# Two moves in the order of work of an expert loop: one on VectorE, one on ScalarE

## The chip, the cores and the metric

The kernel runs on one core of a Trainium2 chip. The metric is the device time of one execution in microseconds (us). Five engines take part: TensorE (PE in the profile, with its weight loads as PEld), VectorE (DVE), ScalarE (ACT), GpSimd (POOL) and SyncE (SP), which here only issues transfers. Each works through its own list of instructions in order and waits on semaphores for the others.

## What is computed

One layer of an encoder for 512 tokens of 2048 numbers: two kinds of attention and a recurrence side by side, a cross attention, and a mixture of experts. The change touches the experts alone, which are, with 32 experts of 512 inner features and two experts per token:

```
def expert_block(args):
    tok, e = args
    xb = x_pad[tok]
    a = jax.nn.silu(xb @ w_gate[e]) * (xb @ w_up[e])
    return a @ w_down[e]
...
y_rows = y_rows.reshape(n_rows, D) * row_w[:, None].astype(y_rows.dtype)
y = jax.ops.segment_sum(y_rows, row_tok, num_segments=N + 1)[:N]
```

All is float32. Each expert has 12 MB of weights and on average 32 rows of tokens.

## The kernel before

**The pieces.** An expert's weights come as 12 pieces of 128 x 2048 numbers, 1 MB each, numbered r: 0 to 3 gate, 4 to 7 up, 8 to 11 down. So the "first gate piece" is r = 0 and the "fourth" is r = 3. Pieces 8 and 9 (`RAW_ONLY`) are multiplied as they land, in float32. The other ten are split in two parts first: ScalarE copies `e_raw` to a rounded `e_hi` (L1399), and VectorE subtracts, `e_lo = e_raw - e_hi` (L1860). TensorE multiplies by both (L1035 and L1036 for gate and up, L1066 and L1067 for down). Both splits are the functions `e_split(b, r)` of the two engines, b being the expert.

**The buffers.** `e_raw`, `e_hi` and `e_lo` have five buffers each for the ten split pieces (`RING = 5`), and `e_raw` has two more for pieces 8 and 9. Piece r of gate and up shares its buffer with piece r - 5, pieces 10 and 11 have those of 3 and 4. SP issues all transfers of weights in one fixed order (L490): before one it waits until VectorE has subtracted the earlier piece of that buffer (`e_lo_done`), and so piece 5 waits for piece 0, and pieces 6 and 7 for 1 and 2. Transfers that are issued queue up and land in that order.

**A round.** The engines run `expert(b, behind, ahead)` for 32 experts, the middle ones in a hardware loop. The order of each engine is written out by hand. The down product of expert b - 1 is worked off in the round of expert b (`behind`), and the first pieces of expert b + 1 are split in it (`ahead`). TensorE's order is: pieces 0 to 5; the transposes of the next expert's rows (L1020); the gate result folded (L1043); pieces 6 and 7; down piece 8 of b - 1 (L1063); the up result folded; down pieces 9, 10 and 11 of b - 1.

**What the change touches.** VectorE's `gate_times_up(b)` forms the product `he` (L1957) from the folded results. It has three waits: `he_silu` from ScalarE, `up_folded` from TensorE, and `e_used` up to piece 9 of b - 1, since TensorE still reads the old `he` for pieces 8 and 9. VectorE's `y_add(b - 1)` adds two halves of the down result into `y_sb` (L1969), one of which ScalarE's `y_low(b - 1)` has copied out of PSUM (L1443). GpSimd then scatters `y_sb` to memory (L657) and gathers the rows of a later expert (L645). On ScalarE `y_low` waits until TensorE has used piece 11. `split_he` makes the parts of `he` that the split down pieces need (L1437, L1962).

Of the kernel before, what the change touches and what calls it, by code (L numbers as in the profile page):

```python
# [63 lines left out]
def layer(nc, x, mem, norm_mix_g, w_in, kv_norm_g, k_idx_norm_g, w_uk, w_uv, conv_w, conv_b, gate_b,  # L64
          ml_norm_g, w_out, norm_x_g, mem_norm_g, w_cq, w_ckv, w_co, norm_ffn_g, w_group, b_group,
          w_router, b_router, w_gate, w_up, w_down, final_norm_g, out):
    with ExitStack() as ctx:
# [85 lines left out]
        def small(name, shape, dt=F32):  # L153
            n = int(np.prod(shape[1:])) * 4
            t = at(name, shape, low[0], dt)
            low[0] += ((n + 31) // 32 * 32) / KB
            assert BASE + low[0] * KB <= nc.sbuf_usable_end, (name, low[0])
            return t
# [71 lines left out]
        more = small("more", [P, NE])  # L230
# [113 lines left out]
        def raw_at(b, r):  # L344
            return e_raw[RAW_LAST[r] if is_last_down(b, r) else RAW[r]]
# [4 lines left out]
        def slot_at(b, r):  # L350
            return SLOT_LAST[r] if is_last_down(b, r) else SLOT[r]
# [17 lines left out]
        def split_count(b, r, more=False):  # L369

            n = r if r < 8 else r - 2
            if more or is_last_down(b, r):
                return b * 10 + (n + 1)
            if r >= 8:
                return b * 10 + (n + 9)
            return n + 1 if isinstance(b, int) and b == 0 else b * 10 + (n - 1)

        def used_count(b, r, more=False):

            if more or is_last_down(b, r):  # L380
                return b * 12 + (r + 1)
            if r >= 8:
                return b * 12 + (r + 9)
            return r + 1 if isinstance(b, int) and b == 0 else b * 12 + (r - 3)
# [718 lines left out]
        def _(act):  # L1103
# [277 lines left out]
            def e_split(b, r, more=False):  # L1381

                act.wait_ge(land_at(b, r), landed(b, r, more))
                first_ = isinstance(b, int) and b == 0 and r < 8
                if first_ and r == 3:
                    act.wait_ge(slot_land, 32)
                    act.wait_ge(more_done, 1)
                    for k in range(2):
                        act.wait_ge(h_store[k], 16 * TT // 2)
                if is_last_down(b, r):  # L1390
                    act.wait_ge(e_used, used_count(b, r - 5))
                elif r >= 8:
                    act.wait_ge(e_used, used_count(b, r - 7, True) if more else used_count(b + 1, r - 7))
                elif r >= RING:
                    act.wait_ge(e_used, used_count(b, r - RING, more))
                elif not first_ and not more:
                    act.wait_ge(e_used, used_count(b - 1, r + RING) if r < 3 else b * 12 + (r - 8))
                n = slot_at(b, r)
                act.activation(e_hi[n][:, :], raw_at(b, r)[:, :], ACT.Copy).then_inc(e_hi_done, 1)  # L1399
# [15 lines left out]
            def rows_out(b):  # L1415

                act.wait_ge(xg_turned, b + 1)
                for k in range(2):
                    act.activation(xt_pair[:, 8 * k:8 * k + 8, 0:BLOCK], psx[2 + k][:, :].rearrange("p (k s) -> p k s", k=8),
                                   ACT.Copy).then_inc(xt_high, 1)  # L1420

            def gate_up(b, more=False):
                for r in range(3, 6):
                    e_split(b, r, more)
                act.wait_ge(e_used, used_count(b, 3, more))
                if not (isinstance(b, int) and b == 0):
                    act.wait_ge(he_done, b)
                act.activation(gu_sb[:, 0, :], psx[0][:, :], ACT.Copy).then_inc(gate_out, 1)
                for r in (6, 7):
                    e_split(b, r, more)  # L1430
                act.wait_ge(gate_folded, b + 1)
                act.activation(he_g[:, :, :], psx[0][:, 0:FT * BLOCK].rearrange("p (f s) -> p f s", f=FT),
                               ACT.Silu).then_inc(he_silu, 1)

            def split_he(b):
                act.wait_ge(he_done, b + 1)
                act.activation(he_pair[:, :, 0:BLOCK], he[:, :, 0:BLOCK], ACT.Copy).then_inc(he_split_a, 1)  # L1437

            def y_low(b, more=False):
                act.wait_ge(e_used, used_count(b, 11, more))  # L1440
                act.wait_ge(put_copied, b + 1)
                for m in range(4):
                    act.activation(y_sb[:, 512 * m:512 * m + 512], psd[m][BLOCK:P, :], ACT.Copy).then_inc(y_low_out, 1)  # L1443

            def expert(b, behind, ahead):
                gate_up(b)
                if behind:
                    e_split(b - 1, 10)
                if ahead:
                    act.wait_ge(e_used, used_count(b, 7))  # L1450
                    rows_out(b + 1)
                if behind:
                    e_split(b - 1, 11)
                if ahead:
                    for r in range(3):
                        e_split(b + 1, r)
                if behind:
                    y_low(b - 1)
                split_he(b)

            rows_out(0)
            expert(0, False, True)
            with act.Fori(1, LAST) as b:
                expert(b, True, True)
            expert(LAST, True, False)
            for r in (10, 11):
                e_split(LAST, r)
# [23 lines left out]
        def _(dve):  # L1491
# [365 lines left out]
            def e_split(b, r, more=False):  # L1857
                dve.wait_ge(e_hi_done, split_count(b, r, more))
                n = slot_at(b, r)
                dve.tensor_tensor(e_lo[n][:, :], raw_at(b, r)[:, :], e_hi[n][:, :].bitcast(F32),  # L1860
                                  ALU.subtract).then_inc(e_lo_done, 1)
# [78 lines left out]
            def rows_out(b):  # L1940
                for k in range(2):
                    dve.wait_ge(xt_high, b * 2 + (k + 1))
                    dve.tensor_tensor(xt_pair[:, 8 * k:8 * k + 8, BLOCK:P],
                                      psx[2 + k][:, :].rearrange("p (k s) -> p k s", k=8),
                                      xt_pair[:, 8 * k:8 * k + 8, 0:BLOCK].bitcast(F32), ALU.subtract).then_inc(xg_out, 1)

            def up_scaled(b, more=False):
                dve.wait_ge(e_used, used_count(b, 7, more))
                dve.tensor_scalar(gu_sb[:, 1, :], psx[1][:, :], slots[:, span(b, 1), 2:3].rearrange("s b c -> s (b c)").bitcast(F32),
                                  None, ALU.mult).then_inc(up_out, 1)  # L1950

            def gate_times_up(b, more=False):
                if not (more or isinstance(b, int) and b == 0):
                    dve.wait_ge(e_used, used_count(b - 1, 9))
                dve.wait_ge(he_silu, b + 1)
                dve.wait_ge(up_folded, b + 1)
                dve.tensor_tensor(he[:, :, 0:BLOCK], psx[1][:, 0:FT * BLOCK].rearrange("p (f s) -> p f s", f=FT),  # L1957
                                  he_g[:, :, :], ALU.mult).then_inc(he_done, 1)

            def split_he(b):  # L1960
                dve.wait_ge(he_split_a, b + 1)
                dve.tensor_tensor(he_pair[:, :, BLOCK:P], he[:, :, 0:BLOCK], he_pair[:, :, 0:BLOCK].bitcast(F32),  # L1962
                                  ALU.subtract).then_inc(he_split_d, 1)

            def y_add(b):
                for m in range(4):
                    dve.wait_ge(y_low_out, b * 4 + (m + 1))
                    y_m = y_sb[:, 512 * m:512 * m + 512]
                    dve.tensor_tensor(y_m, psd[m][0:BLOCK, :], y_m, ALU.add).then_inc(y_out, 1)  # L1969

            def expert(b, behind, ahead):
                for r in range(3, 8):
                    e_split(b, r)
                if behind:
                    e_split(b - 1, 10)
                up_scaled(b)
                if ahead:
                    rows_out(b + 1)
                if behind:
                    e_split(b - 1, 11)  # L1980
                gate_times_up(b)
                if ahead:
                    for r in range(3):
                        e_split(b + 1, r)
                if behind:
                    y_add(b - 1)
                split_he(b)
# [4 lines left out]
            with dve.Fori(1, LAST) as b:  # L1992
                expert(b, True, True)
# [75 lines left out]
```

## Time and profile before

| | us |
|---|---|
| median of 3 runs | 2683.26 |
| lowest and highest | 2680.72 and 2683.41 |
| the profiled execution, its own time | 2688.69 |
| its span, first to last instruction | 2686.9 |
| TensorE busy | 2408.5 |
| VectorE busy | 1529.3 |
| ScalarE busy | 1208.6 |
| GpSimd busy | 319.0 |

The span begins with the dense projections and attention, up to about 1540 us; the experts fill the rest but for the last 60 us. Busy shares over the whole span mix these stages, so the experts have to be read by views of their own stretch. The page cuts the span into 40 slices of 67 us. A digit is the busy share of a slice in tenths. "PEclk" is the granted clock of TensorE in tenths of 2.4 GHz. "GB/s" is what the transfers moved in each slice.

### The profile page before, as it was taken

To read this page: it belongs to the slowest core of one execution; us is meant where nothing else is said; L and a number is where in the kernel's file an instruction comes from. 1 tells how busy PE (TensorE), PEld (TensorE's weight loads), DVE (VectorE), ACT (ScalarE), POOL (GpSimd) and SP (SyncE) were. 2 spreads that over 40 slices of the span, in tenths; PEclk is the share of its full clock that TensorE was granted. 3 is DMA by queue.
4 is the path that set the end of the run, shared out by engine and by line. 5 is a ranking of instruction groups with operands and counts; after the bars stand their busy time and mean duration, and the time that the engine had idled before them with its cause. 6 is when DMAs were issued, how large, how long until landed. Compare 5 with 4: busy or idle time off the path is not lost.

```text
span 2686.9 us, 31537 instructions
## 1 busy us (share of the span) xinstructions
PE 2408.5 (90%) x11141; PEld 1888.5 (70%) x11141; DVE 1529.3 (57%) x1704; ACT 1208.6 (45%) x1376; POOL 319.0 (12%) x182
## 2 busy tenths in 40 slices
PE   6999999899998999999998389999999999999980
PEld 6888588667886889995887266666666666666660
DVE  4322476644234234443233577878887778877775
ACT  4222333443222223443222266666666666666651
POOL 0000000000000000000000122222222222222222
PEclk8999999999998999999999599999999999999995
DMA  4333133103222225650324399999999999999985
GB/s 172 99 96 100 40 97 99 47 24 126 100 88 110 100 93 151 181 163 20 111 94 171 89 371 375 385 381 383 392 385 387 382 383 380 387 380 380 384 326 208
DMA packets 141956, 580.31 MB, mean 216 GB/s; under 512 B 24394, under 2 KB 26704, under 8 KB 86736
## 3 DMA queue, kind: packets, MB, share of 16 engines
q1 hardware_dynamic: 136528, 562.85, 56.6%
q0 software_dynamic: 5376, 16.81, 1.9%
q8 instruction: 28, 0.46, 0.1%
q14 instruction: 24, 0.20, 0.0%
HBM read 571.15 MB, written 25.23 MB: 222 GB/s over the span
## 4 chain that ended last, share of the span: by engine, by line
PE 73%; DVE 17%; issue 6%; DMA 2%; ACT 1%; POOL 0%; DVEq 0%; SPq 0%; POOLq 0%; ACTq 0%
PE psd L722 41%; PE psd L1063 8%; DVE e_lo L1860 8%; PE psx L1035 6%; PE psx L1036 6%; DVE y_sb L1969 3%; PE psx L1020 2%; PE psx L1043 2%; PE psd L970 1%; PE psx L951 1%; PE psd L897 1%; DVE act_lo L1565 1%; PE psd L860 1%; PE psx L786 1%; PE psx L827 1%
## 5 line engine op out<-in xcount | busy, mean ns | idle before, releaser
L1860 DVE TENSOR_TENSOR e_lo<-e_raw,e_hi 128x2048 fp32r<-128x2048 f32 x320 | 718.8, 2287 | 127.0 <-ACT e_hi L1399 127.0
L1504 DVE TENSOR_TENSOR w_lo<-w_raw,w_hi 128x1024 fp32r<-128x1024 f32 (+1 forms) x240 | 291.0, 1213 | 661.0 <-ACT w_hi L1113 661.0
L1399 ACT ACTIVATE e_hi<-e_raw 128x2048 fp32r<-128x2048 f32 x320 | 595.5, 1910 | 32.8 <-DMA e_raw<-in_w_gate_dram 26.1
L1113 ACT ACTIVATE w_hi<-w_raw 128x1024 fp32r<-128x1024 f32 (+1 forms) x240 | 251.9, 1050 | 779.9 <-PE psd L722 779.9
L1035 PE MATMUL psx<-e_hi,xt_pair 128*128 128x512 f32 x1024 | 444.0, 434 | 92.6 <-DVE e_lo L1860 88.0
L1036 PE MATMUL psx<-e_lo,xt_pair 128*128 128x512 f32 x1024 | 429.3, 419 | 0.0
L1035 PEld LDWEIGHTS psx<-e_hi,xt_pair 128*128 128x128 f32 x1024 | 211.4, 206 | 169.7 <-DVE e_lo L1860 119.7
L722 PE MATMUL psd<-w_hi,act_hi 128*128 128x512 f32 (+1 forms) x832 | 320.6, 385 | 6.1 <-DVE act_lo L1565 2.1
L722 PE MATMUL psd<-w_lo,act_hi 128*128 128x512 f32 (+1 forms) x832 | 319.9, 384 | 0.0
L722 PE MATMUL psd<-w_hi,act_lo 128*128 128x512 f32 (+1 forms) x832 | 319.8, 384 | 0.0
L657 POOL DMA_INDIRECT y_rows<-y_sb,put_idx x32 | 208.5, 6515 | 619.0 <-DVE y_sb L1969 619.0
L1036 PEld LDWEIGHTS psx<-e_lo,xt_pair 128*128 128x128 f32 x1024 | 211.2, 206 | 43.7
L1063 PE MATMUL psd<-e_raw,he 128*128 128x512 f32 x512 | 233.3, 599 | 3.4 <-DVE y_sb L1969 3.4
L722 PE MATMUL psd<-act_hi,w_hi 128*128 128x512 f32 x576 | 225.0, 391 | 3.5 <-DVE act_lo L1565 2.0
L722 PE MATMUL psd<-act_hi,w_lo 128*128 128x512 f32 x576 | 224.9, 390 | 0.0
L722 PE MATMUL psd<-act_lo,w_hi 128*128 128x512 f32 x576 | 224.7, 390 | 0.0
L722 PEld LDWEIGHTS psd<-w_hi,act_hi 128*128 128x128 f32 x832 | 157.0, 189 | 37.7 <-issue 2.5
L722 PEld LDWEIGHTS psd<-w_hi,act_lo 128*128 128x128 f32 x832 | 156.9, 189 | 30.2
L722 PEld LDWEIGHTS psd<-w_lo,act_hi 128*128 128x128 f32 x832 | 156.9, 189 | 29.8
L1063 PEld LDWEIGHTS psd<-e_raw,he 128*128 128x128 f32 x512 | 95.3, 191 | 99.5 <-issue 97.1
L722 PEld LDWEIGHTS psd<-act_hi,w_hi 128*128 128x128 f32 x576 | 108.5, 188 | 26.8 <-DVE w_lo L1504 2.3
L722 PEld LDWEIGHTS psd<-act_lo,w_hi 128*128 128x128 f32 x576 | 108.6, 188 | 22.6
(302 smaller groups left out, 2964.9 us busy)
## 6 DMA issues: line engine op xcount, KB each, us to landing
e_raw<-in_w_gate_dram SPq DMA_DIRECT2D x128, 1024.0 KB, 10.7
e_raw<-in_w_up_dram SPq DMA_DIRECT2D x128, 1024.0 KB, 6.1
e_raw<-in_w_down_dram SPq DMA_DIRECT2D x128, 1024.0 KB, 9.8
w_raw<-in_w_in_dram SPq DMA_DIRECT2D x72, 512.0 KB, 3.6
w_raw<-in_w_ckv_dram SPq DMA_DIRECT2D x64, 512.0 KB, 3.6
w_raw<-in_w_out_dram SPq DMA_DIRECT2D x32, 512.0 KB, 3.6
w_raw<-in_w_cq_dram SPq DMA_DIRECT2D x32, 512.0 KB, 3.6
w_raw<-in_w_co_dram SPq DMA_DIRECT2D x32, 512.0 KB, 3.6
```

Source lines behind the costliest of these rows:

```text
L657: pool.indirect_dma_start(out=y_rows[:, :], out_offset=bass.IndirectOffsetOnAxis(ap=put_idx[:, 1:2], axis=0), in_=y_sb[:, :], in_offset=No ...
L722: ins = pe.matmul(o, a, c, start=(kt == 0 and q == 0), stop=(kt == KT - 1 and q == 2))
L1020: ins = pe.transpose(psx[2 + k // 8][:, BLOCK * (k % 8):BLOCK * (k % 8) + BLOCK], xg[:, k:D:KT], ident[0:BLOCK, 0:BLOCK])
L1035: pe.matmul(psx[u][:, :], pair, e_hi[SLOT[r]][:, c], start=(q == 0 and k == 0), stop=False)
L1036: ins = pe.matmul(psx[u][:, :], pair, e_lo[SLOT[r]][:, c], start=False, stop=(q == 3 and k == 3))
L1043: ins = pe.matmul(psx[u][:, BLOCK * f:BLOCK * f + BLOCK], gu_sb[:, u, P * f:P * f + P], fold[:, :], start=True, stop=True)
L1063: ins = pe.matmul(psd[m][:, :], he[:, f, :], raw_at(b, r)[:, c], start=(f == 0), stop=False)
L1113: act.activation(w_hi[j % 2][:, :, 0:w], w_raw[j % 4][:, :, 0:w], ACT.Copy).then_inc(hi_done, 1)
L1399: act.activation(e_hi[n][:, :], raw_at(b, r)[:, :], ACT.Copy).then_inc(e_hi_done, 1)
L1504: dve.tensor_tensor(w_lo[j % 2][:, :, 0:w], w_raw[j % 4][:, :, 0:w], w_hi[j % 2][:, :, 0:w].bitcast(F32), ALU.subtract).then_inc(lo_done, 1)
L1860: dve.tensor_tensor(e_lo[n][:, :], raw_at(b, r)[:, :], e_hi[n][:, :].bitcast(F32), ALU.subtract).then_inc(e_lo_done, 1)
L1969: dve.tensor_tensor(y_m, psd[m][0:BLOCK, :], y_m, ALU.add).then_inc(y_out, 1)
```

## The change

Two moves, and two more lines that keep the order for the first expert and for the rare further blocks as it was.

On VectorE, the subtraction of the next expert's first gate piece (r = 0) is placed ahead of the product `he`; the ones of r = 1 and 2 stay behind it. On ScalarE, the copy of the next expert's fourth gate piece (r = 3) moves from the start of the next round to the end of this one, ahead of `y_low`, the copying of y out of PSUM.

```
@@ class ScalarE: gate_up, expert
             def gate_up(b, more=False):
-                for r in range(3, 6):
+                for r in range(3 if more or isinstance(b, int) and b == 0 else 4, 6):
                     e_split(b, r, more)
...
                 if ahead:
-                    for r in range(3):
+                    for r in range(4):
                         e_split(b + 1, r)
                 if behind:
                     y_low(b - 1)
@@ class VectorE: expert
                 if behind:
                     e_split(b - 1, 11)
+                if ahead:
+                    e_split(b + 1, 0)
                 gate_times_up(b)
                 if ahead:
-                    for r in range(3):
+                    for r in (1, 2):
                         e_split(b + 1, r)
                 if behind:
                     y_add(b - 1)
```

VectorE's instructions in the body of its hardware loop, around the product. `e_lo_135` is the subtraction of piece 11 of b - 1, `e_lo_131` and `e_lo_132` are those of pieces 0 and 1 of b + 1:

```order
 L1860 TENSOR_TENSOR e_lo_135<-e_raw_123,e_hi_130 128x2048
+L1858 ISA
+L1860 TENSOR_TENSOR e_lo_131<-e_raw_119,e_hi_126 128x2048
 L1954 ISA
 L1957 TENSOR_TENSOR he<-psx,he_g 128x4x64
-L1858 ISA
-L1860 TENSOR_TENSOR e_lo_131<-e_raw_119,e_hi_126 128x2048
 L1860 TENSOR_TENSOR e_lo_132<-e_raw_120,e_hi_127 128x2048
```

The subtraction of piece 0 stood right behind the product and stands right ahead of it now; its wait for ScalarE's copy (`e_hi_done`) moves with it.

ScalarE's instructions at the end of its loop body. `e_hi_127` and `e_hi_128` are the copies of pieces 1 and 2 of b + 1, `e_hi_129` is that of piece 3:

```order
 L1399 ACTIVATE e_hi_127<-e_raw_120 128x2048
 L1399 ACTIVATE e_hi_128<-e_raw_121 128x2048
+L1397 ISA
+L1399 ACTIVATE e_hi_129<-e_raw_122 128x2048
 L1440 ISA
 L1443 ACTIVATE y_sb<-psd 64x512 x4
```

The copy of piece 3 is issued ahead of the four copies of y and is gone from the start of the next round, where it stood first. TensorE, SP and GpSimd have the same instructions in the same order as before.

## Rows read from the trace of the kernel before

**Rows 1.** The page: busy time of engines, then 40 slices of the span.

```profile
PE 2408.5 (90%) x11141; PEld 1888.5 (70%) x11141; DVE 1529.3 (57%) x1704; ACT 1208.6 (45%) x1376; POOL 319.0 (12%) x182
...
PEclk8999999999998999999999599999999999999995
DMA  4333133103222225650324399999999999999985
GB/s 172 99 96 100 40 97 99 47 24 126 100 88 110 100 93 151 181 163 20 111 94 171 89 371 375 385 381 383 392 385 387 382 383 380 387 380 380 384 326 208
```

**Rows 2.** One line, the product: count, durations, first and last start; idle time before.

```profile
L1957 DVE TENSOR_TENSOR he<-psx,he_g x32: 424/425/426, 1552.7 to 2606.3; 128x256 f32<-128x256 f32 x32
...
  PE psd L1063: 77.2, 31
```

**Rows 3.** Stretches: length, busy PE, PEld, DVE, ACT, POOL; PEclk, DMA share, GB/s.

```profile
1924.88:1960.28 35.40, 32.59 (x129) 23.72 (x128) 27.38 (x20) 22.66 (x19) 9.23 (x4) 0.90 1.00 386
1960.28:1993.23 32.95, 29.97 (x129) 21.28 (x128) 27.28 (x19) 20.95 (x19) 10.03 (x4) 1.00 0.97 369
...
1936.88:1940.28 3.40, 3.40 (x9) 2.62 (x10) 3.40 (x2) 0.00 (x0) 3.40 (x1) 0.54 1.01 424
```

**Rows 4.** VectorE in order of time, one round: start, length, what, [idle before, releaser].

```profile
1960.28 0.42 DVE L1957 TENSOR_TENSOR he<-psx,he_g 128x256 f32<-128x256 f32 x1 [2.48 <-PE psd L1063]
1960.62 6.69 DVE L1860 TENSOR_TENSOR e_lo<-e_raw,e_hi 128x2048 fp32r<-128x2048 f32 x3
1967.22 2.47 DVE L1969 TENSOR_TENSOR y_sb<-psd,y_sb 64x512 f32<-64x512 f32 x4
...
1969.94 6.69 DVE L1860 TENSOR_TENSOR e_lo<-e_raw,e_hi 128x2048 fp32r<-128x2048 f32 x3
...
1988.47 2.29 DVE L1860 TENSOR_TENSOR e_lo<-e_raw,e_hi 128x2048 fp32r<-128x2048 f32 x1 [0.34 <-ACT e_hi L1399]
1993.23 0.42 DVE L1957 TENSOR_TENSOR he<-psx,he_g 128x256 f32<-128x256 f32 x1 [2.47 <-PE psd L1063]
```

**Rows 5.** TensorE in that round: a matmul with its wait, then the chain.

```profile
1972.28 0.50 PE L1035 MATMUL psx<-e_hi,xt_pair 128*128 128x512 f32 x1 [2.81 <-DVE e_lo L1860]
...
1989.71 3.50 PE psd L1063 x8
```

**Rows 6.** The 2 us behind one product; then 2 to 5 us behind six successive ones.

```profile
1960.28:1962.28 2.00, 2.00 (x10) 1.65 (x9) 2.00 (x2) 1.92 (x1) 0.00 (x0) 1.00 1.00 418
...
1926.88:1929.88 3.00, 3.00 (x15) 2.49 (x14) 3.00 (x3) 1.51 (x4) 0.00 (x0) 1.00 0.91 325
1962.28:1965.28 3.00, 3.00 (x15) 2.48 (x14) 3.00 (x3) 1.36 (x3) 0.00 (x0) 1.00 0.65 205
1995.23:1998.23 3.00, 3.00 (x15) 2.49 (x14) 3.00 (x3) 2.66 (x3) 0.00 (x0) 1.00 0.99 412
2030.62:2033.62 3.00, 3.00 (x15) 2.49 (x14) 3.00 (x3) 1.35 (x3) 0.00 (x0) 1.00 0.56 167
2063.58:2066.58 3.00, 3.00 (x15) 2.49 (x14) 3.00 (x3) 1.36 (x3) 0.00 (x0) 1.00 0.92 311
2098.91:2101.91 3.00, 3.00 (x15) 2.49 (x14) 3.00 (x3) 1.36 (x3) 0.00 (x0) 1.00 0.43 104
```

**Rows 7.** Transfers issued at 1963.06 and, the second, at 1951.88: KB, us to landing.

```profile
e_raw<-in_w_up_dram SPq DMA_DIRECT2D x1, 1024.0 KB, 4.8
...
e_raw<-in_w_gate_dram SPq DMA_DIRECT2D x1, 1024.0 KB, 10.9
```

**Rows 8.** ScalarE in order of time, the same round.

```profile
1960.33 1.92 ACT L1399 ACTIVATE e_hi<-e_raw 128x2048 fp32r<-128x2048 f32 x1 [0.51 <-DMA e_raw<-in_w_gate_dram]
...
1963.91 2.06 ACT L1443 ACTIVATE y_sb<-psd 64x512 f32<-64x512 f32 x4 [1.67 <-PE psd L1067]
...
1966.16 5.51 ACT L1399 ACTIVATE e_hi<-e_raw 128x2048 fp32r<-128x2048 f32 x3
...
1990.10 1.91 ACT L1399 ACTIVATE e_hi<-e_raw 128x2048 fp32r<-128x2048 f32 x1 [1.66 <-DMA e_raw<-in_w_gate_dram]
```

More of the change, by code:

```diff
@@ L1422, in gate_up @@
             def gate_up(b, more=False):
-                for r in range(3, 6):
+                for r in range(3 if more or isinstance(b, int) and b == 0 else 4, 6):
                     e_split(b, r, more)
@@ L1454, in expert @@
                 if ahead:
-                    for r in range(3):
+                    for r in range(4):
                         e_split(b + 1, r)
@@ L1980, in expert @@
                     e_split(b - 1, 11)
+                if ahead:
+                    e_split(b + 1, 0)
                 gate_times_up(b)
                 if ahead:
-                    for r in range(3):
+                    for r in (1, 2):
                         e_split(b + 1, r)
```

## The prediction

> **What bounds the kernel now.** The page comes first. TensorE is busy 90% of the span, VectorE 57%. In the last 17 of the 40 slices, the experts, the DMA share stands at its top digit but for the end and the rate at some 384 GB/s, against 20 to 181 before them [rows 1]. So the experts are the one stretch in which everything is nearly full, and the change touches them alone. A view of one line gives their rhythm: the product `he` (L1957) runs 32 times, first at 1552.7 and last at 2606.3, so a round of one expert takes (2606.3 - 1552.7) / 31 = 33.99 us. VectorE idles 77.2 us before 31 of these products, 2.5 us each, until TensorE has finished with the old `he` [rows 2].
>
> Then two rounds side by side, from product to product [rows 3]. One takes 32.95 us at clock 1.00, the other 35.40 us at 0.90. Rounds of the two lengths take turns for most of the stretch. The clean one first, on VectorE [rows 4]: product at 1960.28, three subtractions of the next expert's first pieces (1960.62 to 1967.22, 2.20 us apart), four additions of y and the small `he` piece until 1969.94, then the subtraction of the fourth piece. TensorE has run dry by then: it waits 2.81 us for that subtraction and starts at 1972.28 [rows 5]. From there it runs without a wait to the end of the second down piece (1989.71 and 3.50 us) [rows 5], which lets the next product go at 1993.23 [rows 4]. The round is thus VectorE's 12 us after the product and TensorE's 21 us, and it is closed by the product that waited.
>
> In the long round the stretch right behind the same wait is granted 0.54 of the clock, the 1.2 GHz level for nearly all of it [rows 3]. What the wait costs through the clock is read from the two rounds: 35.40 - 32.95 = 2.45 us, every other time.
>
> Last the transfers. A round moves 384 GB/s x 33.99 us = 13.1 MB: 12 pieces of 1.05 MB, and 0.5 MB of rows of tokens. In six successive rounds, of both lengths, the stretch from 2 to 5 us behind the product moves 325, 205, 412, 167, 311 and 104 GB/s [rows 6]. The queue runs empty there, since the sixth piece may be fetched only when the first one's buffer is free, that is, after its subtraction. A piece issued there (1963.06) lands in 4.8 us, where one in a full queue takes 10.9 [rows 7].
>
> **The product behind the next first piece's subtraction.** Nothing is added or removed: 31 times one VectorE instruction changes place with another. In the clean round the last subtraction before the product starts at 1988.47, so the next could start 2.20 us later, at 1990.67, and be over by 1992.9. The product runs at 1993.23 anyhow [rows 4]. So the 2.47 us of idle time take the subtraction in, and all that follows the product on VectorE comes 2.20 us earlier. The condition is that ScalarE's copy `e_hi` of this piece is ready by 1990.7. In this round it is not: ScalarE waited 1.66 us for the landing and ended at 1990.10 + 1.91 = 1992.0 [rows 8]. The subtraction would end at 1994.3, the product would be 1.1 us late, and the gain there is 1.1 us. Who waits for a late product: ScalarE's `he_pair`, and later `gu_sb` and the second four pieces on TensorE, all over 5 us away, so only VectorE's own order counts. So the gain of the chain lies between 1.1 and 2.20 us per round.
>
> **The fourth gate piece's copy ahead of y.** Again one move, 1.91 us long (1.80 from start to start, 5.51 us for three) [rows 8]. ScalarE has 1.67 us free before the copies of y at 1963.91. The copy of the third piece ends at 1962.25. The fourth piece was issued at 1951.88 and lands in about 10.9 us, at 1962.8 [rows 7]. Its copy then runs to 1964.7, the copies of y start 0.7 us late, and the first is over at some 1965.2. The additions of y on VectorE start at 1967.22 now and could start at 1965.02 after the first move. So they lose 0.2 us. What the move buys is that the copy of the fourth piece is ready when VectorE comes to it, at 1967.9 instead of 1969.94. Without the move that would be at 1967.7, but ScalarE would end the copy at 1966.16 + 1.91 = 1968.1. So the move is worth some 0.2 us net (1968.1 less 1967.9), and nothing if the landing is late. No DMA is moved on SP or POOL. SP's waits on `e_lo_done` stay the same numbers, and come true earlier; the rows of y go to POOL earlier.
>
> **The new chain, and what is late next.** Clean: 32.95 - 2.20 + 0.2 = 30.95 us, or 32.1 where the first piece lands late. TensorE is busy 29.97 us of a clean round [rows 3], so it would be nearly full. But the transfers have their own floor. What the hole costs is its shortfall against 418 GB/s, the rate of the 2 us between one product and its hole [rows 6]. (418 - rate) / 418 x 3 us gives 0.67, 1.53, 0.04, 1.80, 0.77 and 2.25, in the mean 1.18 us. The sixth piece's fetch comes 2.2 to 2.9 us earlier by the first move, and the next two 2.2 us. That fills the hole. The other time of the queue stays: it works for 33.99 - 1.18 = 32.8 us per round, among it the gathered and scattered rows, at less than the full rate. That is above the chain's 30.95, so **the transfers decide**: a round of 32.8 us.
>
> The sum: 31 rounds x 1.18 = 36.5 us. The profiled execution took 2688.69 us, 5.4 above the median of 2683.26 and 1.8 above its own span of 2686.9. So 2652 on its terms and 2647 against the median. I take **2647**.
>
> A word on the share of 0.97 to 1.00 [rows 3]. By itself it would say that 0.03 of 33.99 us, 1 us, is all there is, or nothing in a long round. The rate says more, since 369 to 386 stand against 418 at best [rows 3, 6]. The Trainium skill (Perfetto Trace Analysis, Identifying the Most-Contended Engine) holds with the rate: for DMA it wants the use of HBM bandwidth, not occupancy, as sixteen engines make occupancy misleading. The trace agrees in part: 0.91 of share goes with 325 GB/s in the first hole of [rows 6]. By occupancy alone the gain would be 0 to 31 us and the sum 2652 to 2683, by the rate it is the 2647 above.
>
> **The rivals.**
> *The transfers have no floor at 32.8* (chance 0.17). Once the queue is never empty, the slow parts could go too. Then (384 / 418) x 33.99 = 31.2 us, and the chain gives 30.95. Taking 31.2, that is 2.8 us x 31 = 86 us, so 2597, and 2622 halfway to the forecast. For it: the clock of the long rounds may come back. Against: rows of tokens are moved each round.
> *The clock drops in every round* (0.16). The wait on TensorE moves from the fourth subtraction to landings, and is spread. If half clock comes each time, the chain is 30.95 + 2.45 = 33.4 to 33.6 with late landings, 0.4 to 0.6 below now: 2665 to 2671. The Trainium skill (TensorE: Matmul & The Clock Gate, HAM oscillation) tells of a loop that waits for a DMA at each tile and finds TensorE cold each time. That speaks for this rival; this trace has the drop in every other round only [rows 3].
> *No change* (0.08). If the transfers are the bound already, as the share says, VectorE's earlier work only waits for landings: 2678 to 2688.
> *Slower* (0.07). ScalarE is in order, so the copies of y now stand behind a landing. It decides when the fourth piece lands so late that the additions of y start later than now: 1967.22 - 0.59 - 1.80 = 1964.8, 4.5 us behind the product, where it is 2.5 now. A queue deeper by one piece (2.5 us) would pass this point by 0.5 us, by two pieces by 3. At 1 us per round this is 31 us and **2714**. For it: ScalarE already waits for the second and third landing in these places [rows 8]. Against: the chain can only lag as long as the transfers are behind, and these gain.
>
> **How the numbers follow.** The forecast case has 0.52 and its own range is 2638 to 2658. The range of 8 in 10 takes in the clock rival above and most of the lower one below: 2604 to 2671. Left out are no change, slower and the lower edge, 0.19. A measurement of this kernel tells 0.2% (5 us) from no change. Faster 0.85, same 0.08, slower 0.07.
>
> **What the profile after would show.** VectorE's idle time before L1957 falls from 77 us to under 20. The stretch from 2 to 5 us behind the product moves 380 GB/s or more. TensorE's wait for the fourth subtraction falls from 2.8 us to about 1, and ScalarE's idle time on landings of `e_raw` rises, since the transfers are the bound. If the wait before L1957 stays, `e_hi` of the first piece was late. If the hole is filled and the round is under 32 us, the floor was wrong; if the copies of y start later than 5 us behind the product, the second move costs.

## The result and the profile after

| | before | after |
|---|---|---|
| median, us (4 runs each) | 2681.99 | 2636.16 |
| lowest and highest | 2679.92 to 2683.41 | 2634.64 to 2638.78 |
| the profiled execution's span | 2686.9 | 2635.3 |

The changed kernel is faster by 45.8 us. The ratio is 0.9831, with a 95% interval of 0.9814 to 0.9848. The forecast was 2647 in a range of 2604 to 2671.

The page after, its slices of the clock and of the transfers:

```profile
PEclk9999999999998999999999689999999999999995
DMA  4333133102222224660321579999999999999985
GB/s 172 103 97 96 40 96 96 64 25 112 96 96 109 98 90 134 183 183 33 102 96 64 193 256 404 407 409 403 399 395 396 406 398 405 403 390 397 402 350 213
```

In the experts' slices the rate was 371 to 392 GB/s [rows 1] and is 390 to 409 now. The busy digit did not move, since it stood at the top before. All of the gain lies there. The view of the product's line answers to [rows 2]: count, durations, first and last start, then the idle time before it and what ended that.

```profile
L1957 DVE TENSOR_TENSOR he<-psx,he_g x32: 415/424/425, 1553.8 to 2556.1; 128x256 f32<-128x256 f32 x32
...
  PE psd L1063: 6.6, 16
```

A round is (2556.1 - 1553.8) / 31 = 32.33 us, where it was 33.99. The 31 rounds give 51.3 us, nearly the whole difference of the two profiled spans, 51.6. (The profiled execution of before, at 2688.69 us, was 6.7 us above the median in the table, so the two profiles differ by more than the medians do.) VectorE's idle time before the product went from 77.2 to 6.6 us.

The order in one round after, on VectorE, then on ScalarE, in order of time: start, length, what, idle time before and its releaser.

```profile
2102.19 0.42 DVE L1957 TENSOR_TENSOR he<-psx,he_g 128x256 f32<-128x256 f32 x1
2102.52 4.49 DVE L1860 TENSOR_TENSOR e_lo<-e_raw,e_hi 128x2048 fp32r<-128x2048 f32 x2
2107.87 2.48 DVE L1969 TENSOR_TENSOR y_sb<-psd,y_sb 64x512 f32<-64x512 f32 x4 [0.86 <-ACT y_sb L1443]
...
2110.60 6.68 DVE L1860 TENSOR_TENSOR e_lo<-e_raw,e_hi 128x2048 fp32r<-128x2048 f32 x3
...
2129.96 4.49 DVE L1860 TENSOR_TENSOR e_lo<-e_raw,e_hi 128x2048 fp32r<-128x2048 f32 x2 [0.34 <-ACT e_hi L1399]
2134.71 0.42 DVE L1957 TENSOR_TENSOR he<-psx,he_g 128x256 f32<-128x256 f32 x1 [0.26 <-PE psd L1063]
```

```profile
2102.74 1.92 ACT L1399 ACTIVATE e_hi<-e_raw 128x2048 fp32r<-128x2048 f32 x1 [0.48 <-DMA e_raw<-in_w_gate_dram]
2105.29 1.92 ACT L1399 ACTIVATE e_hi<-e_raw 128x2048 fp32r<-128x2048 f32 x1 [0.64 <-DMA e_raw<-in_w_gate_dram]
2107.24 2.05 ACT L1443 ACTIVATE y_sb<-psd 64x512 f32<-64x512 f32 x4
```

Against [rows 4] the product is preceded without a gap worth the name by two subtractions, and two follow it instead of three. Against [rows 8] the fourth piece's copy stands ahead of the copies of y. It waited 0.64 us for its landing, so the copies of y started at 2107.24, 5.05 us behind the product, and VectorE waited 0.86 us for them. The subtraction of the fourth piece began 8.4 us behind the product. It was 9.7 before, and 7.5 would be the least.

Six successive stretches from 2 to 5 us behind the product, the counterpart of [rows 6], and three whole rounds, that of [rows 3]. The columns are the length, the five busy times, the clock, the DMA share and GB/s.

```profile
1906.30:1909.30 3.00, 3.00 (x15) 2.49 (x14) 2.83 (x2) 2.42 (x3) 0.00 (x0) 1.00 0.95 369
1939.95:1942.95 3.00, 2.80 (x13) 1.84 (x11) 2.91 (x2) 2.36 (x2) 0.00 (x0) 1.00 1.04 393
1973.41:1976.41 3.00, 3.00 (x15) 2.48 (x14) 2.88 (x2) 2.36 (x2) 0.00 (x0) 1.00 1.00 407
2006.61:2009.61 3.00, 3.00 (x15) 2.49 (x14) 2.81 (x2) 2.37 (x2) 0.00 (x0) 1.00 0.91 358
2040.72:2043.72 3.00, 3.00 (x15) 2.48 (x14) 3.00 (x3) 2.98 (x4) 0.00 (x0) 1.00 1.01 393
2071.51:2074.51 3.00, 3.00 (x15) 2.48 (x14) 2.82 (x2) 2.35 (x2) 0.00 (x0) 1.00 1.04 431
2038.72:2069.51 30.79, 29.84 (x129) 21.36 (x128) 27.29 (x20) 21.69 (x19) 10.69 (x4) 1.00 1.00 398
2069.51:2102.19 32.68, 30.83 (x134) 22.18 (x133) 27.30 (x20) 22.96 (x20) 8.57 (x4) 1.00 1.01 410
2102.19:2134.71 32.52, 29.81 (x125) 21.75 (x124) 27.36 (x20) 22.53 (x20) 8.26 (x4) 0.95 1.01 404
```

The hole is filled: the mean of the six is 392 GB/s where it was 254, and over the 30 rounds from the second product on it is 405 where it was 245. The rounds no longer come in two lengths. Apart from the first and the last, the shortest are 30.8 us, and most lie between 31.5 and 34.

### The profile page after: what moved, and what is told of

It reads as the page before. It is cut to its first block, busy times and chain, and to the rows that moved or that the text cites. A ratio compares the mean times of both kernels' runs of the same rounds, so it can differ in the third digit from the quotient of the medians.

```text
span 2635.3 us, 31537 instructions
## 1 busy us (share of the span) xinstructions
PE 2382.7 (90%) x11141; PEld 1869.6 (71%) x11141; DVE 1531.6 (58%) x1704; ACT 1217.0 (46%) x1376; POOL 303.1 (12%) x182
## 3 DMA queue, kind: packets, MB, share of 16 engines
q1 hardware_dynamic: 136528, 562.85, 57.1%
## 4 chain that ended last, share of the span: by engine, by line
PE 59%; DMA 17%; DVE 13%; issue 6%; ACT 4%; POOL 0%; DVEq 0%; SPq 0%; ACTq 0%; POOLq 0%
PE psd L722 42%; DMA e_raw<-in_w_gate_dram 8%; DMA e_raw<-in_w_down_dram 7%; DVE e_lo L1860 5%; PE psx L1035 2%; PE psx L1036 2%; PE psd L1063 2%; ACT e_hi L1399 2%; DVE y_sb L1969 1%; PE psd L970 1%; PE psx L1020 1%; PE psx L951 1%; PE psx L1043 1%; ACT y_sb L1443 1%; PE psd L897 1%
## 5 line engine op out<-in xcount | busy, mean ns | idle before, releaser
L1399 ACT ACTIVATE e_hi<-e_raw 128x2048 fp32r<-128x2048 f32 x320 | 601.9, 1912 | 87.8 <-DMA e_raw<-in_w_gate_dram 63.0
L1035 PE MATMUL psx<-e_hi,xt_pair 128*128 128x512 f32 x1024 | 428.3, 418 | 67.0 <-DVE e_lo L1860 60.9
L1036 PE MATMUL psx<-e_lo,xt_pair 128*128 128x512 f32 x1024 | 415.6, 406 | 0.0
L1035 PEld LDWEIGHTS psx<-e_hi,xt_pair 128*128 128x128 f32 x1024 | 202.4, 198 | 141.9 <-DVE e_lo L1860 95.0
L1036 PEld LDWEIGHTS psx<-e_lo,xt_pair 128*128 128x128 f32 x1024 | 202.4, 198 | 40.8
L722 PEld LDWEIGHTS psd<-act_hi,w_lo 128*128 128x128 f32 x576 | 108.1, 188 | 22.5
```

What stands on the lines that cost most here:

```text
L722: ins = pe.matmul(o, a, c, start=(kt == 0 and q == 0), stop=(kt == KT - 1 and q == 2))
L1035: pe.matmul(psx[u][:, :], pair, e_hi[SLOT[r]][:, c], start=(q == 0 and k == 0), stop=False)
L1036: ins = pe.matmul(psx[u][:, :], pair, e_lo[SLOT[r]][:, c], start=False, stop=(q == 3 and k == 3))
```

## The experiments

In all of them the change of time is given as the ratio to the kernel before, with its 95% interval.

### Each move alone

The first move only, on VectorE:

```
                 if behind:
                     e_split(b - 1, 11)
+                if ahead:
+                    e_split(b + 1, 0)
                 gate_times_up(b)
                 if ahead:
-                    for r in range(3):
+                    for r in (1, 2):
                         e_split(b + 1, r)
```

> Only the first move: on VectorE the subtraction of the next first gate piece stands ahead of the product, ScalarE is as before. Theory (the empty stretch of the queue behind the product is filled, then the transfers set a round of 32.3 to 32.8 us): nearly all of the gain, 2634 to 2645 us, VectorE idle before L1957 under 20 us. Rival (the second move is needed, since the fourth piece's copy is late otherwise): 2650 to 2665 us, TensorE's wait for the fourth subtraction over 2 us.

Measured: 2636.99 us, ratio 0.9832 (0.9815 to 0.9849). That is all of the gain. VectorE's idle time, in the same view of the product's line:

```profile
L1957 DVE TENSOR_TENSOR he<-psx,he_g x32: 414/418/425, 1548.1 to 2551.2; 128x256 f32<-128x256 f32 x32
...
  PE psd L1063: 4.2, 7
```

Its rounds are (2551.2 - 1548.1) / 31 = 32.36 us, those of the kernel with both moves (32.33) within 0.03.

The second move only, on ScalarE:

```
             def gate_up(b, more=False):
-                for r in range(3, 6):
+                for r in range(3 if more or isinstance(b, int) and b == 0 else 4, 6):
                     e_split(b, r, more)
...
                 if ahead:
-                    for r in range(3):
+                    for r in range(4):
                         e_split(b + 1, r)
```

> Only the second move: on ScalarE the copy of the next fourth gate piece stands ahead of the copies of y, VectorE is as before. Theory: the additions of y still start 6.9 us behind the product, later than the copies of y in nearly all rounds, so no change: 2677 to 2687 us. Rival (copies of y behind a landing cost time): 2690 to 2715 us.

Measured: 2682.6 us, ratio 0.9999 (0.9988 to 1.001). The product's line reads as before:

```profile
L1957 DVE TENSOR_TENSOR he<-psx,he_g x32: 424/425/426, 1544.4 to 2599.1; 128x256 f32<-128x256 f32 x32
...
  PE psd L1063: 76.5, 31
```

So the first move does it all, and the second alone does nothing either way. The rival that the copies of y lose time behind a landing fell too, for this order of VectorE's work.

### What the clock costs

The kernel before and the changed one, each with matmuls that nobody needs behind the third gate piece. There TensorE waits anyhow, and the bank is free:

```
                     ins.then_inc(e_used, 1)
+                    if r == 2 and not more:
+                        for _ in range(8):
+                            pe.matmul(psx[2][:, :], xt_pair[:, 0, :], xt_pair[:, 0:4, :], start=True, stop=True)
```

> The kernel before, with 8 matmuls of 128x512 behind each third gate piece, into a free bank (their result is not used), some 1.8 of the 2.8 us for which TensorE waits there. It measures what the drop of the clock costs, which was read as 2.45 us in every other round. Theory: no stretch at 0.54, every round 33.0 us, 2645 to 2655 us. Rival (the long rounds have another cause, such as the transfers): 2675 to 2690 us.

Measured on the kernel before: 2654.95 us, ratio 0.9895 (0.9878 to 0.9913). Whole rounds, and then the stretches from 2 to 5 us behind six products:

```profile
2044.45:2077.41 32.96, 31.77 (x137) 22.79 (x136) 27.19 (x20) 23.19 (x20) 8.56 (x4) 1.00 1.01 399
2077.41:2110.41 33.00, 31.83 (x137) 22.79 (x136) 27.25 (x19) 23.35 (x20) 8.54 (x4) 1.00 1.00 397
2110.41:2143.37 32.96, 31.78 (x137) 22.78 (x136) 27.29 (x19) 22.12 (x20) 8.57 (x4) 1.00 1.00 399
...
2046.45:2049.45 3.00, 3.00 (x15) 2.48 (x14) 3.00 (x3) 2.98 (x4) 0.00 (x0) 1.00 0.99 380
2079.41:2082.41 3.00, 3.00 (x15) 2.48 (x14) 3.00 (x3) 2.70 (x4) 0.00 (x0) 1.00 0.94 350
2112.41:2115.41 3.00, 3.00 (x15) 2.49 (x14) 3.00 (x3) 2.23 (x4) 0.00 (x0) 1.00 0.97 377
2145.37:2148.37 3.00, 3.00 (x15) 2.48 (x14) 3.00 (x3) 2.98 (x4) 0.00 (x0) 1.00 0.99 388
2178.55:2181.55 3.00, 3.00 (x15) 2.49 (x14) 3.00 (x3) 2.97 (x4) 0.00 (x0) 1.00 0.99 363
2211.51:2214.51 3.00, 3.00 (x15) 2.49 (x14) 3.00 (x3) 2.72 (x4) 0.00 (x0) 1.00 0.82 287
```

The rounds of over 35 us are gone. From the second product to the last, the kernel before has 30 stretches at half clock and this one has one, in a round of 34.6 us. The price of 2.45 us is borne out in the main: before, 13 of 31 rounds were of over 35 us, 13 x 2.45 = 32 us, and 27.6 were gained, with three rounds of 33.9 to 34.6 us left over. There is more in it. Most of the hole in the queue went as well, though VectorE does its work in the old order and the sixth piece is issued as late as ever, 2.8 us behind the product. The mean of the six is 357 GB/s against 254, that of 30 rounds 363 against 245. So the late buffer by itself makes a shallow hole. The deep ones go with the long rounds: in [rows 6] the deep holes (205, 167 and 104) are those of the clean rounds, each of which follows a long one. The reading that fits is that the transfers get ahead in a long round and have too little left to fetch in the next. How far ahead they are was not measured by itself.

> The changed kernel, with 4 such matmuls (0.9 us) behind each third gate piece. Theory (the transfers set the round): the few stretches at half clock go, but the time stays within 0.3%, 2630 to 2640 us. Rival (the clock is what is left to gain): 2610 to 2625 us.

Measured on the changed kernel, with 4 matmuls instead of 8: 2637.29 us, against 2636.16 without them, ratio 0.9843 (0.9826 to 0.986). Its experts, as one stretch of the windows view:

```profile
1587.00:2555.00 968.00, 921.52 (x3916) 664.29 (x3914) 811.44 (x561) 677.16 (x559) 262.96 (x116) 0.99 1.01 402
```

The clock is up from 0.97 to 0.99, and the stretches at half clock, counted as above, are down from 14 in the changed kernel to 7, not to none as expected. Nothing came of it in time.

### Are the transfers the bound?

The second down piece of the looped experts is fetched by half. The same edit was made on both kernels:

```
                     dst = raw_at(b, r)[:, :]
+                    if r in (9,) and not isinstance(b, int):
+                        src, dst = src[:, 0:D // 2], dst[:, 0:D // 2]
                 sp.dma_start(dst, src).then_inc(land_at(b, r), 16)
```

> The kernel before, but the second down piece of the looped experts is fetched by half: 0.5 MB less per round, 1.25 us of the queue at 418 GB/s (those experts' results are not the reference's). Theory (before, engines set the round and the queue has room): 2674 to 2684 us. Rival (the transfers were the bound already): 2640 to 2650 us.

Measured: 2682.26 us, ratio 0.9999 (0.9986 to 1.0011). Half a MB less is worth nothing there. The rate of the queue simply falls, from 384 to 368 GB/s, and the hole gets deeper, from 245 to 171 GB/s in the mean of 30 rounds:

```profile
1600.00:2500.00 900.00, 824.91 (x3368) 593.66 (x3368) 719.14 (x501) 594.39 (x501) 247.98 (x106) 0.95 0.95 368
```

> The changed kernel with the same piece fetched by half. Theory (the transfers set its round of 32.3 us): the round falls by 1.1 to 1.25 us, to the chain's 31, 2598 to 2606 us. Rival (the engines or the clock set it): 2628 to 2638 us.

Measured: 2602.35 us, ratio 0.9699 (0.9678 to 0.9719), 33.8 us under the changed kernel. That is 1.1 us per round, against 1.25 for the bytes. Its windows view:

```profile
1600.00:2500.00 900.00, 861.46 (x3653) 617.41 (x3653) 779.57 (x542) 648.21 (x541) 249.89 (x113) 0.99 1.01 399
```

The clock rose here too, from 0.97 to 0.99, but the run with 4 extra matmuls had the same rise and gained nothing. The same edit that gives nothing before the change gives nearly its whole price after it, so the bound has moved from the engines to the transfers. With both raw pieces fetched by half (`r in (8, 9)`):

> The changed kernel with the first and the second down piece fetched by half: 1 MB less per round, 2.5 us. It measures the chain of the engines by itself. Theory: every round 30.95 us (worked out before), 2590 to 2597 us, no half clock, and little less than with one half piece. Rival (there is no such second floor): 2558 to 2570 us, twice the gain of one half piece.

Measured: 2585.11 us, ratio 0.965 (0.9623 to 0.9677), 17 us less again and a little below the expected range of 2590 to 2597. The second half MB gives half as much as the first, as the engines take over. Its product line:

```profile
L1959 DVE TENSOR_TENSOR he<-psx,he_g x32: 418/425/426, 1546.4 to 2499.7; 128x256 f32<-128x256 f32 x32
```

(2499.7 - 1546.4) / 31 = 30.75 us, and 26 of the 31 rounds take 30.8. That is the chain of the engines without the transfers, which the prediction put at 30.95.

### What the second move is worth

The first move alone, with the same two half pieces, so that the transfers don't hide what the chain does:

> The first move only, with the two down pieces fetched by half as before (1 MB less per round). With the transfers out of the way it shows what the second move is worth in the chain of the engines. Theory (the copy of the fourth piece ends 8.1 us behind the product instead of before 7.5, worked out as 0.2 us net): rounds of 31.1 to 31.4 us, 2590 to 2605 us, 5 to 20 above the same kernel with both moves (2585). Rival (the second move gives nothing or costs): 2575 to 2587 us.

Measured: 2604.05 us, ratio 0.9709 (0.968 to 0.9739), 18.9 us above the same kernel with both moves. The kernel before took 2685.20 us beside this run and 2682.61 beside the other, and the two ratios, 0.9709 and 0.965, differ by 16 us. The intervals just don't touch. VectorE in one typical round, without and then with the second move:

```profile
2078.06 0.42 DVE L1959 TENSOR_TENSOR he<-psx,he_g 128x256 f32<-128x256 f32 x1 [0.27 <-PE psd L1065]
2078.40 4.48 DVE L1862 TENSOR_TENSOR e_lo<-e_raw,e_hi 128x2048 fp32r<-128x2048 f32 x2
2082.80 2.47 DVE L1971 TENSOR_TENSOR y_sb<-psd,y_sb 64x512 f32<-64x512 f32 x4
...
2085.90 2.29 DVE L1862 TENSOR_TENSOR e_lo<-e_raw,e_hi 128x2048 fp32r<-128x2048 f32 x1 [0.29 <-ACT e_hi L1401]
```

```profile
2007.03 0.42 DVE L1959 TENSOR_TENSOR he<-psx,he_g 128x256 f32<-128x256 f32 x1 [0.27 <-PE psd L1065]
2007.37 4.49 DVE L1862 TENSOR_TENSOR e_lo<-e_raw,e_hi 128x2048 fp32r<-128x2048 f32 x2
2011.77 2.47 DVE L1971 TENSOR_TENSOR y_sb<-psd,y_sb 64x512 f32<-64x512 f32 x4
...
2014.50 2.28 DVE L1862 TENSOR_TENSOR e_lo<-e_raw,e_hi 128x2048 fp32r<-128x2048 f32 x1
```

The fourth subtraction starts 7.84 us behind the product without the move, waiting 0.29 us for ScalarE, and 7.47 us with it, without a wait. The additions of y start 4.74 us behind the product in both. Most rounds are of 31.14 and of 30.8 us, 0.34 us apart. The rest of the 0.5 to 0.6 us per round goes with the clock: six rounds of 32.7 us without the move have a stretch at half clock, against one of 32.6 us with it. At 1.6 us each the five more rounds are 8 us over the kernel. In the real kernel none of this shows, since the transfers bind.

### What the gather costs the queue

The changed kernel, with the gather of token rows bounded to row 0:

```
-                    bounds_check=T - 1, oob_is_err=False).then_inc(xg_land, 16)
+                    bounds_check=0, oob_is_err=False).then_inc(xg_land, 16)
```

> The changed kernel, whose gather of token rows takes row 0 alone, so nearly nothing is moved and the experts work on zeros. Some 0.25 MB less per round, 0.6 us at 418 GB/s. Theory (the slow stretch of the queue 25 to 29 us behind the product, at 307 to 354 GB/s, is the gather's doing): 1.4 to 1.7 us less per round, down to the chain's 31, 2592 to 2606 us. Rival (the gather costs its bytes alone): 2614 to 2622 us.

Measured: 2590.75 us, ratio 0.9658 (0.9623 to 0.9692), 45.4 us under the changed kernel or 1.46 us per round, just under the expected 2592 to 2606. The page's rows of the weights' queue (q1) and of the software queue (q0), which carries gather and scatter, after the change and without the gather:

```profile
q1 hardware_dynamic: 136528, 562.85, 57.1%
q0 software_dynamic: 5376, 16.81, 2.0%
```

```profile
q1 hardware_dynamic: 136528, 562.85, 57.0%
q0 software_dynamic: 5376, 8.44, 0.9%
```

The software queue moves 8.4 MB less, 0.26 MB per expert, which at 418 GB/s would be 0.62 us. So the gather takes more than twice its bytes from the queue. The shares say where: of the spans of 2635.3 and 2591.7 us, the software queue's packets took some 29 us less without the gather, 0.9 us per expert, and those of the weights, the same bytes, some 27 us less (57.1% against 57.0%), another 0.9 us. It can be seen in the changed kernel. In the 5 us in which the gathered rows are under way, 24 to 29 us behind the product, the share stays at the top and the rate is low:

```profile
2093.80:2098.80 5.00, 5.00 (x19) 2.64 (x18) 5.00 (x5) 3.35 (x4) 0.00 (x0) 1.00 1.01 346
2126.19:2131.19 5.00, 5.00 (x21) 2.97 (x20) 4.66 (x5) 4.16 (x4) 0.00 (x0) 1.00 1.01 316
```

Rounds come down to the chain's 30.8 there, so 1.46 us is a lower bound. Why the gather slows the weights beside it, and what the scatter costs, is open: no kernel without the scatter was run.

## Why the prediction was right, step by step

**The bound after the change.** "The transfers decide" was the main step, and it holds: half a MB less gives 33.8 us after the change and nothing before it. A round of 32.8 us was forecast and 32.33 came. The chain behind it was worked out as 30.95 us and measured as 30.8.

**The size of the gain.** This term was mis-sized: 1.18 us per round for the hole, where the profile of after shows 1.66 (33.99 - 32.33), or 1.48 by the medians (45.8 / 31). The 1.18 us for the hole itself was right. What failed is the sentence "The other time of the queue stays". The queue was slow behind the hole as well. From 9 to 11 us behind the product, six successive rounds before the change gave 311, 307, 381, 393, 397 and 336 GB/s, and six after it 426, 414, 426, 434, 402 and 418. The shortfall against 418 was 0.31 us per round there and has gone. In the mean of the 30 rounds from the second product on, in GB/s:

| us behind the product | before | after | gained at 418 GB/s, us |
|---|---|---|---|
| 2 to 5 | 245 | 405 | 1.15 |
| 5 to 9 | 413 | 393 | -0.19 |
| 9 to 11 | 337 | 420 | 0.40 |
| 18 to 20 | 365 | 417 | 0.25 |

That is 1.6 us together, and the other stretches change by 0.1 us or less each. The first move alone has 419 GB/s in the stretch of 9 to 11 us. The kernel before with the extra matmuls still has 341 there, so that part is not the clock's. Why the queue was slow from 9 to 11 and from 18 to 20 us stays open.

**Why the hole was there.** The prediction named the late buffer of the sixth piece. That is what the queue waited for, but it is not the main cause. Matmuls that keep TensorE's clock up filled some 60% of the hole ((357 - 254) / (418 - 254)) without any piece being issued earlier. So most of it went with the alternation of long and clean rounds, for which the prediction's sum has no term. That its 1.18 us came out right does not show its reason right. With the changed kernel the stretches at half clock fell from 30 to 14, while TensorE's wait ahead of the fourth piece fell from 2.7 to 1.9 us in the mean. That the shorter wait made them rarer fits, but no run shows it by itself. Of the 45.8 us, 27.6 are to be had by the clock alone. The other 18 take the shorter chain, which lets the rounds fall from 33.07 us, the mean of the fill kernel, to the floor of the transfers. How the gain of the changed kernel itself divides between clock and chain was not measured.

**The first move.** The subtraction fitted into the idle time, as forecast (77.2 to 6.6 us of idle), and alone gives the whole gain. The first piece did land late in rounds (the product waited for TensorE in 16 of 31 only, so in the others it followed its subtraction straight on). What that costs was not measured; the transfers bind either way.

**The second move.** It was put at 0.2 us net in the chain and nothing by the transfers. It gives nothing in the kernel (2636.99 without, 2636.16 with it), and 0.5 to 0.6 us per round where the transfers are relieved. There the chain's part of 0.34 us is the prediction's 0.4 us, the copy ready at 1968.1 where VectorE comes at 1967.7. The 0.2 us that the additions of y were to lose did not come, since they start 4.74 us behind the product in both kernels.

**The rivals.** That the transfers have no floor fell with the halved pieces. That the clock drops in every round fell: the clock's mean over 1600 to 2500 us rose from 0.95 to 0.97. Its price was also added up too low: the prediction's own 32.1 us for late landings with 2.45 us is 34.55, not 33.6, and so slower than before. That the change does nothing fell, and with it the reading of the DMA share: at 0.98 of share there were 1.5 us per round to be had. The slower case, the copies of y behind a landing, is real as a mechanism: they start 5.05 us behind the product in the round shown and 5.08 in the median of 30, and make VectorE wait, 28.6 us over the kernel. But it waits for what binds anyhow.

**What the profile was to show.** The idle time before L1957 under 20 us: yes. The hole at 380 GB/s or more: 392 in the mean, 358 at the least. ScalarE's wait for landings up: it went from 31 to 77 us. TensorE's wait for the fourth subtraction down to about 1 us: no, it fell from 84.7 to 57.5 us in 31 waits, from 2.7 to 1.9 us each. The landings and the copies of y come before it: with the transfers relieved it is 23.3 us in 29 waits, 0.8 us each. The copies of y later than 5 us behind the product, as a sign that the second move costs: they are, by a little, and it costs nothing.

## What to carry to other kernels

An idle stretch of an in-order engine that waits for the last reader of its output is a place for the next independent instruction. What that is worth depends on what binds next, so work out the chain and the floor of the transfers apart and take the longer. A queue that runs dry in every second round is best read together with the length of the round before it: a stall elsewhere may have let it get ahead. To ask whether transfers bind, fetch one piece by half: that gave 0 before the change and 33.8 us after it, while the busy share read 0.98 and 1.01. And when a slow stretch of a queue is counted as gain, look through the whole round for others.

## What was not expected of the hardware

With a wait of 2.8 us of TensorE once per round, nearly every other round had stretches at half clock and was 2.45 us longer, 13 of 31. Eight useless matmuls of 1.8 us in that wait made the kernel before 1.05% faster (2682.54 to 2654.95 us, ratio 0.9895). A gather of 0.26 MB into a full queue took 1.46 us of it or more, against 0.62 us for its bytes, and the packets of the weights beside it took longer too.
